# Residual additions of six sublayers on GpSimd, with VectorE scaling three chunks ahead of the next norm

## What is computed

```python
def _ffn_sublayer(h, mod, g_pre, g_post, w_in, w_out):
    shift, scale, gate = mod
    u = _modulate(_rmsnorm(h, g_pre), shift, scale)      # rmsnorm(h) * g_pre * (1 + scale) + shift
    a, b = jnp.split(u @ w_in, 2, axis=-1)
    y = (jax.nn.silu(a) * b) @ w_out
    return h + MACARON_W * gate * _rmsnorm(y, g_post)
```

## Time and profile before

| what | value |
|---|---|
| median of 3 executions | 2326.97 us (2326.83 to 2328.91) |
| the profiled execution | 2327.34 us, span of its trace 2325.3 us |
| PE busy | 2246.1 us, 97% |
| DVE busy | 1460.8 us, 63% |
| ACT busy | 1016.2 us, 44% |
| POOL busy | 33.4 us, 1% |
| chain that ended last | PE 82%, DVE 9%, ACT 3%, issue 3% |

### The profile page before, as it was taken

One profiled execution on the slowest core, in us unless ns is written; L12 is line 12 of the kernel. 1 busy time (PEld: TensorE's weight loads), 2 busy tenths in 40 slices (PEclk: granted clock), 3 DMA queues, 4 the chain that ended last, 5 costly groups with the idle time before them and its releaser, 6 DMA issues.

```text
span 2325.3 us, 39346 instructions
## 1 busy us (share of the span) xinstructions
PE 2246.1 (97%) x14002; PEld 1913.1 (82%) x14002; DVE 1460.8 (63%) x2101; ACT 1016.2 (44%) x1479; POOL 33.4 (1%) x35
## 2 busy tenths in 40 slices
PE   6999999999999999999999999999899989999998
PEld 5888888788777888888788888788799989989897
DVE  4774577776667872777532234776764577856765
ACT  5322224544456332225432234645554457455553
POOL 0000000000000000000000000000000000000000
PEclk9999999999989999999999999999999999999999
DMA  9664555322133753655333425442255645215321
GB/s 329 196 177 134 156 174 172 114 69 68 42 91 100 208 170 109 183 164 151 91 86 93 110 83 158 118 113 75 93 161 168 180 141 153 75 40 162 100 74 55
DMA packets 399397, 298.64 MB, mean 128 GB/s; under 512 B 13342, under 2 KB 361252, under 8 KB 399140
## 3 DMA queue, kind: packets, MB, share of 16 engines
q1 hardware_dynamic: 365322, 231.58, 34.3%
q10 hardware_dynamic: 33946, 65.35, 8.6%
HBM read 295.84 MB, written 1.06 MB: 128 GB/s over the span
## 4 chain that ended last, share of the span: by engine, by line
PE 82%; DVE 9%; ACT 3%; issue 3%; DMA 1%; SPq 1%; DVEq 0%; ACTq 0%; POOL 0%; POOLq 0%
PE banks L1076 24%; PE banks L1077 23%; PE banks L1078 23%; PE banks L1342 2%; ACT wh L1840 1%; DVE wl L2511 1%; DVE uR L2457 1%; PE banks L1176 1%; DVE yT L2630 1%; DVE hT L2635 1%; PE banks L1207 1%; PE banks L1293 1%; DMA big<-in_ada_w 1%; PE banks L1285 1%; PE banks L882 1%
## 5 line engine op out<-in xcount | busy, mean ns | idle before, releaser
L1076 PE MATMUL banks<-uR,wh 128*128 128x512 f32 (+1 forms) x2368 | 830.0, 350 | 19.0 <-DVE uR L2457 14.0
L1077 PE MATMUL banks<-uR,wh 128*128 128x512 f32 (+1 forms) x2368 | 814.6, 344 | 0.0
L1078 PE MATMUL banks<-uR,wl 128*128 128x512 f32 (+1 forms) x2368 | 814.1, 344 | 0.0
L2511 DVE TENSOR_TENSOR wl<-wraw,wh 128x2048 fp32r<-128x2048 f32 (+2 forms) x202 | 423.8, 2098 | 325.4 <-ACTq L1768 314.6
L1840 ACT ACTIVATE wh<-wraw 128x2048 fp32r<-128x2048 f32 (+4 forms) x208 | 367.0, 1764 | 427.8 <-PE banks L1078 369.9
L1076 PEld LDWEIGHTS banks<-uR,wh 128*128 128x128 f32 x2368 | 452.1, 191 | 91.2 <-issue 21.3
L1078 PEld LDWEIGHTS banks<-uR,wl 128*128 128x128 f32 x2368 | 452.0, 191 | 52.9
L1077 PEld LDWEIGHTS banks<-uR,wh 128*128 128x128 f32 x2368 | 452.6, 191 | 49.4 <-issue 0.5
L1076 PE MATMUL banks<-gR,wh 128*128 128x512 f32 (+1 forms) x704 | 256.9, 365 | 2.9 <-DVEq L2362 2.6
L1077 PE MATMUL banks<-gR,wh 128*128 128x512 f32 (+1 forms) x704 | 255.3, 363 | 0.0
L1078 PE MATMUL banks<-gR,wl 128*128 128x512 f32 (+1 forms) x704 | 255.2, 362 | 0.0
(11 more groups left out here) (343 smaller groups left out, 2375.3 us busy)
## 6 DMA issues: line engine op xcount, KB each, us to landing
wraw<-in_ffn_w_in SPq DMA_DIRECT2D x176, 512.0 KB, 5.1
ada_buf<-in_ada_w ACTq DMA_DIRECT2D x24, 1280.0 KB, 6.0
wraw<-in_w_in SPq DMA_DIRECT2D x56, 512.0 KB, 4.7
wraw<-in_ffn_w_out SPq DMA_DIRECT2D x64, 384.0 KB, 4.2
wraw<-in_ffn_w_out SPq DMA_DIRECT2D x64, 320.0 KB, 4.6
ada_buf<-in_ada_w ACTq DMA_DIRECT2D x24, 768.0 KB, 4.5
wraw<-in_da_w_in SPq DMA_DIRECT2D x24, 512.0 KB, 4.6
wraw<-in_na_w_in SPq DMA_DIRECT2D x24, 512.0 KB, 4.6
```

The costliest lines, as they stand in the source:

```text
L1076: mm(o, a[0], b[0], start=first, stop=False)
L1077: mm(o, a[0], b[1], start=False, stop=False)
L1078: return mm(o, a[1], b[0], start=False, stop=last)
L2511: do(V.tensor_tensor(wl[:, s, 0:n], wraw[:, s, 0:n], wh[:, s, 0:n].bitcast(F32), ALU.subtract), w_lo)
```

## The change

The addition moves from DVE's queue to POOL's. DVE signals each scaled chunk by `res_scaled`; POOL waits for it, adds, and signals `res_added`; DVE's `norm(k)` waits for that. DVE scales chunks 0, 1 and 2 ahead of the first norm and from then on chunk k+3 behind norm(k) and low(k-1), where it was k+2.

```diff
@@ gpsimd
-            var = Tally()
+            var, res = Tally(), Tally()
...
                     root((T - c0) // P)
                     root((T - c0) // P, 4 + c0 // P)
+                    for k in range(DC):
+                        pool.wait_ge(res_scaled, res.up())
+                        nc.gpsimd.tensor_tensor(hT[:, k, c0:T], hT[:, k, c0:T], yT[:, k, c0:T], ALU.add).then_inc(res_added, 1)
@@ vector, residual
-                scaled, added = [], []
 
                 def scale(k):
                     if k == DC - 1:
                         dve.wait_ge(gy_ready, tl["gy"].up())
-                    V.tensor_tensor(yT[:, k, c0:T], yT[:, k, c0:T], r[:, 0:T - c0], ALU.mult).then_inc(vec_step, 1)
-                    scaled.append(own.up())
-
-                def add(k):
-                    dve.wait_ge(vec_step, scaled[k])
-                    V.tensor_tensor(hT[:, k, c0:T], hT[:, k, c0:T], yT[:, k, c0:T], ALU.add).then_inc(vec_step, 1)
-                    added.append(own.up())
+                    V.tensor_tensor(yT[:, k, c0:T], yT[:, k, c0:T], r[:, 0:T - c0], ALU.mult).then_inc(res_scaled, 1)
 
                 scale(0)
                 dve.wait_ge(root_ready, tl["root"].up())
                 two_parts(old, nt)
-                add(0)
                 scale(1)
+                scale(2)
                 if feed and c0:
                     dve.wait_ge(n1_half, tl["cols"].up())
                     rest_columns(b, 0, w_half)
                 rs, free2 = product(small)
                 for k in range(DC):
-                    dve.wait_ge(vec_step, added[k])
+                    dve.wait_ge(res_added, tl["added"].up())
                     norm(to, c0, streams, k, rs)
                     if k:
                         low(to, streams, k - 1)
-                    if k + 1 < DC:
-                        add(k + 1)
-                    if k + 2 < DC:
-                        scale(k + 2)
+                    if k + 3 < DC:
+                        scale(k + 3)
                 low(to, streams, DC - 1)
```

More of the change, by code:

```diff
@@ L367, in build @@
         root_ready = sem("root_ready")
+        res_scaled = sem("res_scaled")
+        res_added = sem("res_added")
         diag_ready = sem("diag_ready")
@@ L2353, in _ @@
             tl = {k: Tally() for k in ("root", "wide", "silu", "exp", "pv", "aa", "sq", "sq2", "copy", "gy", "split", "uh", "gh", "ada", "half", "sums",
-                                       "tail", "cols", "landed0", "landed1")}
+                                       "tail", "cols", "landed0", "landed1", "added")}
             V = nc.vector
```

## The result

The changed kernel takes **2334.27 us** (median of 14 executions, 2331.84 to 2337.28), the kernel before beside it on the same chip 2328.65 us (14, 2326.83 to 2330.48). The ratio is 1.0025, 95% interval 1.0018 to 1.0032: slower by 5.6 us, and the whole interval lies above one. Predicted were 5.7 us more than the median of before.

A forecast was written before the change was run, and what follows sets the result against it. VectorE was taken to pace the six handovers at 2.41 us a chunk, ACT and TensorE close behind. With turns taken, 0.8 + 0.8 + 1.2 + 0.2 + 1.2 + 1.5 = +5.7 us gave 2332.7 us, range 2316 to 2341.

The forecast's parts named there:

- Turns taken, the whole instruction: Handovers: DVE's two-SBUF-input operations and POOL's adds exclude each other for the whole instruction; +5.7 us in all, chance 0.50.
- The addition's price: POOL's add in the handovers: 1.2 us wide (0.91 to 1.43), 0.8 narrow (0.65 to 0.91).
- The step: Wide handover, per chunk: low, scale, add and two hops take 2.56 us against 2.41; four steps +0.6 us.
- two_parts: Start of handovers: the root's subtraction may wait 1.2 us behind the first add or nothing; 0.5 counted in each wide handover.
- The start at 714 and 1099: Up to the first low, adds 0 to 3 back to back plus two_parts: +1.2 us at 714, +0.8 at 1099.
- The gain behind the last addition: Wide handovers' last three steps, without adds, run at PE's 2.07 us: 6.2 us for 6.89, so -0.6.
- The handover at 1692: All 256 wide: steps of 1.64 us for 1.34, start and two_parts +0.5 each, last steps -1.0; total +1.2.
- The handover at 1901: A wide subtraction before the first norm takes its turn with add 1: start +1.3, then +1.2 - 1.0; total +1.5.
- The clock, costed at nothing: PE's slow 1.2 GHz stretch after idling at 1901: a longer wait moves it, assumed not to lengthen it; 0 us.
- The first rival: Handovers: DVE and POOL hinder each other only 0.05 us, PE sets the pace; -9.8 us, 2317.2; chance 0.33.
- The add as the bound: Handovers: POOL's add so slow that norm(k) stops DVE's queue; about +24 us at 2.9 us an add, 2351; chance 0.10.
- Given back: Behind the handovers weights or ACT bind, so neither gain nor loss arrives; 2327 us; chance 0.07.

The follow-up runs named there:

- both edits: Changed kernel with two_parts ahead of the first scale and GpSimd's addition of chunk k+3 released by low of chunk k: 2319.06 us, ratio 0.9960.
- the three useless operations: Kernel before plus eight unneeded GpSimd operations in each of the first five handovers: addition 2354.99, copy 2333.55, memset 2329.51 us.
- the first edit: Changed kernel with two_parts (the split of the root) moved ahead of the first scale: 2330.16 us, ratio 1.0006.

## Why the prediction was right, point by point

- **Who bounds the handover**: VectorE, at 2.41 us a chunk, with ACT and TensorE close behind. Right for the four wide handovers, not for the narrow one at 1692 (below). Without additions, and with both edits, low comes every 2.0 to 2.1 us.
- **Turns taken, the whole instruction**: right, and shown by taking the overlap away and by the three useless operations. The 0.05 us of the earlier trace rows was no measure of its size; that a reader of four elements was felt at all was the sign. The power there was under way for 1.01 us and cost 0.05, while an addition costs nearly all that is left of it. What was weighed against the row, the Trainium skill's page SBUF — State Buffer, section "Who interferes with whom", has both of what the runs showed: a VectorE instruction with two SBUF inputs contends with a GpSimd one that reads SBUF, and not with one that only writes it. The page calls the shared ports an exclusive lock; that the first to issue holds them for the whole instruction it says of VectorE's 2-port modes, and the prediction took it over to these instructions. The trace agrees but for 0.15 us: 1.40 us for 0.69, where 0.86 of the addition was left. The power's 0.05 us is not explained by it.
- **The addition's price**: 1.2 us taken, 1.28 measured; narrow 0.8, and 0.72 to 0.74 measured in 15 of 16 (the mean of 0.79 holds one of 1.71 that was itself blocked by a VectorE subtraction). The 4497 ns that the Trainium skill (GPSIMD Engine Reference, section 3.1) has for 2048 elements gave an estimate of 1.12 by proportion to size; the trace has 0.16 more. By the same estimate the narrow one is 0.56, and the steps alone would have made the sum some 3 us smaller, where the prediction has 2. The bounds of 0.91 and 1.43 held it.
- **The step**: 2.56 taken, 2.52 measured from one low's end to the next, four times +0.11 against 2.41 instead of +0.15. The hop from scale to addition, a guess of 0.08, is 0.08 (a scale ends at 431.25, the addition starts at 431.33). The dearer addition was made up for by low's own streaming: it overlaps the addition's end by a little (it ends 0.54 us after it, not 0.69).
- **two_parts**: I counted 0.5 of 1.2 in each, not knowing who gets in first. GpSimd won all six times, in the first handover by 0.03 us: 1.24 or 1.25 us for 0.16 in four, 0.70 in the two narrow ones. The +0.3 for the four additions of the start didn't come on top: low(0) waited for ACT until 429.96 and the fourth addition was done at 429.97. Together the first low stands 6.70 us behind the first scale, for 5.62: +1.08 where 0.8 was summed. So this term was undersized by half, and the first edit, which takes it away and with it the lower clock at 1099 (below), was worth 4 us.
- **The start at 714 and 1099**: +1.2 and +0.8 were summed up to the first low, and +1.85 and +2.38 came. Beyond the 1.08 of two_parts this is the clock, below.
- **The gain behind the last addition**: -0.6 taken, and right. On TensorE chunks 4 to 7 take 6.30 us (440.80 to 447.10) for 6.89, and -0.63 and -0.65 at 714 and 1099. VectorE's own lows win 1.15 us there, of which TensorE could use half.
- **The handover at 1474**: +0.2 taken; +0.43 at TensorE's eighth chunk, with -1.14 behind the last addition where -1.2 was taken.
- **The handover at 1692**: +1.2 taken, -0.05 on TensorE and +0.10 at VectorE's last low, behind which the weights' subtraction stands that the prediction had on the path. This is the term that failed. VectorE's step is 1.42 us and not 1.64, for 1.33, since the narrow addition is shorter and low is done 0.28 us after it:

```profile
1702.48 0.84 DVE L2462 TENSOR_TENSOR uR<-yT,uR 128x256 fp32r<-128x256 f32 x1
...
1703.91 0.83 DVE L2462 TENSOR_TENSOR uR<-yT,uR 128x256 fp32r<-128x256 f32 x1
```

Here two_parts and the four additions of the start cost +0.54 together and not +1.0, and the last steps gave back 0.8. TensorE doesn't wait for VectorE here: before as after, it begins its first chunk 1.9 us behind the first low's start, and the last six chunks go at 1.08 us each, under VectorE's step.
- **The handover at 1901**: +1.5 taken, +1.04 at TensorE's eighth chunk, of which +0.98 are there at the first. The wide subtraction does take its turn with the additions, 1.64 us for 1.22, and the first norm comes 0.95 us later where +1.3 was taken.
- **The clock, costed at nothing**: this was wrong. In the handover at 1099 the loss is +2.20 us, nearly three times the term. TensorE's timeline there, before:

```profile
1099.87 1.11 PE L949 MATMUL banks<-identR,rootR 128*128 128x128 f32 x8 [0.75 <-DVEq L2362]
1100.90 0.86 PE L882 MATMUL banks<-ada_buf,silu_c 128*32 128x128 f32 x24
...
1102.47 1.74 PE L882 MATMUL banks<-scratch,silu_c 128*32 128x128 f32 x56
```

and after:

```profile
1103.00 1.76 PE L951 MATMUL banks<-identR,rootR 128*128 128x128 f32 x8 [1.83 <-DVEq L2367]
1104.69 1.51 PE L884 MATMUL banks<-ada_buf,silu_c 128*32 128x128 f32 x24
...
1107.04 3.20 PE L884 MATMUL banks<-scratch,silu_c 128*32 128x128 f32 x56
```

The granted clock of these stretches, busy times of PE, PEld, DVE, ACT, POOL, then the clock; first before, from 1095.4 to 1105.3:

```profile
1095.40:1105.30 9.90, 7.65 (x157) 6.44 (x155) 8.21 (x21) 4.90 (x11) 1.79 (x2) 1.00 0.39 108
```

and after, from 1097.4 to 1110.4:

```profile
1097.40:1110.40 13.00, 10.50 (x157) 8.70 (x156) 9.47 (x21) 5.61 (x12) 7.03 (x7) 0.74 0.30 82
```

TensorE idled 1.83 us for the delayed root where it had idled 0.75, and the same small products behind it took 1.51 for 0.86 and 3.20 for 1.74: the granted clock is at its lower level, 1.2 GHz, for part of the stretch. ACT copies the result of the 24 products before it makes the next input, and idled 7.12 us in front of that, for 4.73, low(0) waits 2.16 us for ACT, and TensorE, still at the slow products, takes up the first chunk 0.86 us after low(0) is done, where it had waited for it. With the split in front, where the idle time is 0.39 us, the clock of this place is back at 1.00 and the products at 0.86 and 1.74. At 714 the first norm waits 0.69 us for TensorE, whose eight products take 1.97 us for 1.11, and the granted clock is 0.71 from 710.4 to 722.0, for 0.83 before from 710.0 to 720.0. At 424 it fell as well, to 0.85 from 1.00, but there VectorE was the later one again by the fifth chunk and nothing of it was left. But the idle time isn't the only condition: in the kernel before, at 1474, the 56 products take 3.22 us after an idle 0.75 too. What decides it stays open.

The difference of +5.7 came out within 0.1 us of the measured +5.6, partly by luck. (The predicted time, 2332.7, stands 1.6 below 2334.27, since it was reckoned from the median of before's first three executions, 2326.97, and fourteen have 2328.65.) The start was too small in the four wide handovers and the clock was missing, which gave +5.3 there for 3.0 taken; the two narrow ones were too large, +1.0 for 2.7 taken. The two errors cancel but for 0.6 us, and a further 2.1 us behind the handovers stand against -2.4 elsewhere in the span, for which no term stands. The mechanism, and the sign in the wide handovers, didn't depend on them. That moving work off VectorE gains nothing because of reads, and that apart from them it gains 9, is shown; how the median's 5.6 us divides among the six handovers isn't, since only one execution of each kernel was profiled.

**The first rival** (side by side, 2317.2) missed on the kernel as changed and hit the one with both edits, 2319.06. Its parts, -1.9, -1.9, -1.9, -2.2, -1.5 and -0.4, stand beside -1.8, -1.1, -1.8, -1.9, -0.9 and -0.3 of the kernel with both edits and -1.9, -1.1, -1.9, -2.3, -0.5 and -0.6 of the kernel without additions. **The add as the bound** fell with 1.28 us. **Given back** fell too: the gain does reach the end where it is made.

## What to carry to other kernels

Before moving work from VectorE to GpSimd, sort VectorE's operations by where their operands lie: those with one operand in PSUM kept their 0.68 us beside every addition here, those with two in SBUF were stretched by a GpSimd addition and by a copy, and not by a memset. Then let the release of GpSimd's operation set the phase: here one more wait turned +5.6 us into -2.4, and with a tiny subtraction put ahead of the first addition into -9. And look for a block in durations, not in idle time: a 0.16 us operation that lasts 1.24 is the whole finding.

## What was unexpected of the hardware

- The blocked instruction is recorded as busy, on either engine: low 1.40 for 0.69, the copy on GpSimd 1.04 for 0.62. The waits view doesn't show it at all, and VectorE's busy share stays at 63%.
- A blocked low ends 0.54 to 0.55 us after GpSimd's operation, be it an addition (435.70 against 435.16) or a copy (435.23 against 434.69), 0.14 less than its duration alone. So it loses a little less than the rest of the other.
- GpSimd on 128x512 fp32: addition 1.28 us, copy 0.62, memset 0.53. On 128x256 an addition that nothing blocks takes 0.72 to 0.74. From the two sizes of the useless addition (1281 and 732 ns) I estimate 2.1 ns a column and 0.18 us fixed, so the fixed 0.39 taken from the powers was too high and the streaming price too low.
- An idle 1.1 us longer on TensorE, ahead of small products, went with a lower granted clock behind it and about doubled them; in two of four wide handovers a stall of a root by one GpSimd addition thus cost more than its own 1.08 us (up to the first low 1.85 and 2.38).
